# Sliding-window attention: a float32 value product against two passes over split operands, with the output halves added per head

## The reference, cut to what matters

```python
def sliding_window_attention(q, k, v, sinks, slopes):
    ...
    logits = jnp.einsum('bnqkgd,bnskd->bnkgqs', qb, kk).astype(jnp.float32) * scale
    ...
    logits = logits - sl * dist.astype(jnp.float32)
    logits = jnp.where(valid[None, :, None, None], logits, -jnp.inf)
    ...
    p = jax.nn.softmax(jnp.concatenate([logits, sink], axis=-1), axis=-1)[..., :-1]
    out = jnp.einsum('bnkgqs,bnskd->bnqkgd', p.astype(v.dtype), vv)
    return out.reshape(b, s, SW_WIDTH)

def odd_layer(h, w_in, b_in, sinks, w_out):
    ...
    o = sliding_window_attention(q, k, v, sinks, alibi_slopes(SW_HEADS))
    return (o * jax.nn.silu(g)) @ w_out
```

## Time and profile before

| what | value |
|---|---|
| median of 3 runs | 1840.45 us (1839.17 to 1842.74) |
| profiled execution, its time | 1845.26 us |
| its span in the profile | 1843.5 us |
| PE (TensorE matmul) busy over the span | 1673.8 us (91%) |
| DVE (VectorE) busy | 1060.7 us (58%) |
| ACT (ScalarE) busy | 823.3 us (45%) |
| last attention: first score matmul to end of the last value product | 1647.35 to 1767.69 us |

### The profile page before, as it was taken

One profiled execution on the slowest core, in us unless ns is written; L12 is line 12 of the kernel. 1 busy time (PEld: TensorE's weight loads), 2 busy tenths in 40 slices (PEclk: granted clock), 3 DMA queues, 4 the chain that ended last, 5 costly groups with the idle time before them and its releaser, 6 DMA issues.

```text
span 1843.5 us, 24067 instructions
## 1 busy us (share of the span) xinstructions
PE 1673.8 (91%) x8860; PEld 1412.3 (77%) x8860; DVE 1060.7 (58%) x1760; ACT 823.3 (45%) x1544; POOL 93.4 (5%) x112
## 2 busy tenths in 40 slices
PE   7998999998999999989999998889987979979977
PEld 6886787886778888868798896668765758859965
DVE  5557877674545656552254438864465984446654
ACT  5545665663334455541132226652353542235641
POOL 2000400000000000000000001100000100000001
PEclk9998999999999999999999999988997989989988
DMA  6411122113431333322223320111320111320011
GB/s 184 125 50 30 46 63 64 46 52 110 141 120 47 101 104 91 91 92 67 99 74 99 108 81 25 35 46 41 102 84 21 47 46 47 99 69 24 28 42 46
DMA packets 147870, 132.95 MB, mean 72 GB/s; under 512 B 8560, under 2 KB 142448, under 8 KB 147776
## 3 DMA queue, kind: packets, MB, share of 16 engines
q1 hardware_dynamic: 143744, 119.58, 21.3%
q0 software_dynamic: 3136, 10.78, 1.6%
q10 hardware_dynamic: 896, 1.32, 0.3%
HBM read 124.33 MB, written 7.34 MB: 71 GB/s over the span
## 4 chain that ended last, share of the span: by engine, by line
PE 74%; DVE 15%; ACT 5%; issue 5%; DMA 1%; DVEq 0%; ACTq 0%; POOL 0%
PE bank L292 19%; PE bank L293 19%; PE bank L294 19%; DVE wlo L285 2%; PE bank L1206 2%; PE bank L1220 2%; ACT whi L278 1%; PE bank L1189 1%; PE bank L2911 1%; DVE ptl L1374 1%; DVE sz L2700 1%; PE bank L2870 1%; PE bank L1223 1%; PE bank L2278 1%; PE bank L2883 1%
## 5 line engine op out<-in xcount | busy, mean ns | idle before, releaser
L292 PE MATMUL bank<-hh,whi 128*128 128x512 f32 (+3 forms) x1208 | 466.2, 386 | 16.0 <-DVE wlo L285 5.6
L293 PE MATMUL bank<-hl,whi 128*128 128x512 f32 (+3 forms) x1208 | 455.7, 377 | 0.0
L294 PE MATMUL bank<-hh,wlo 128*128 128x512 f32 (+3 forms) x1208 | 455.2, 377 | 0.0
L278 ACT ACTIVATE whi<-wraw 128x2048 fp32r<-128x2048 f32 x111 | 212.1, 1913 | 338.6 <-PE bank L294 338.5
L285 DVE TENSOR_TENSOR wlo<-wraw,whi 128x2048 fp32r<-128x2048 f32 x111 | 254.1, 2289 | 178.7 <-ACT whi L278 177.3
L292 PEld LDWEIGHTS bank<-hh,whi 128*128 128x128 f32 (+2 forms) x1208 | 231.2, 191 | 60.9 <-issue 5.8
L294 PEld LDWEIGHTS bank<-hh,wlo 128*128 128x128 f32 (+2 forms) x1208 | 230.5, 191 | 43.3
L293 PEld LDWEIGHTS bank<-hl,whi 128*128 128x128 f32 (+2 forms) x1208 | 231.2, 191 | 39.1 <-issue 0.7
L1374 DVE TENSOR_TENSOR ptl<-bank,pth 128x128 fp32r<-128x128 f32 (+3 forms) x128 | 56.8, 485 | 64.4 <-ACT pth L1282 63.0
L292 PE MATMUL bank<-ah,whi 128*128 128x512 f32 (+1 forms) x224 | 83.8, 374 | 10.6 <-DVE al L3046 8.3
L292 PE MATMUL bank<-yh,whi 128*128 128x512 f32 (+1 forms) x220 | 79.3, 360 | 6.7 <-DVE yl L1740 6.7
(11 more groups left out here) (393 smaller groups left out, 3212.2 us busy)
## 6 DMA issues: line engine op xcount, KB each, us to landing
wraw<-in_w_in_a_dram SPq DMA_DIRECT2D x52, 512.0 KB, 4.5
wraw<-in_w_up_dram SPq DMA_DIRECT2D x42, 512.0 KB, 4.9
wraw<-in_w_in_dram SPq DMA_DIRECT2D x34, 512.0 KB, 4.8
wraw<-in_w_in_c_dram SPq DMA_DIRECT2D x18, 512.0 KB, 4.7
wraw<-in_w_down_dram SPq DMA_DIRECT2D x16, 512.0 KB, 4.0
wraw<-in_w_out_a_dram SPq DMA_DIRECT2D x16, 512.0 KB, 4.0
aside<-stage POOLq DMA_DIRECT2D x20, 256.0 KB, 2.3
wraw<-in_w_attn_br_dram SPq DMA_DIRECT2D x8, 512.0 KB, 4.0
```

The costliest lines, as they stand in the source:

```text
L278: act.activation(whi[:, p], wraw[:, p], ACT.Copy).then_inc(w_hi_done, 1)
L292: pe.matmul(out, ws[0], hs[0], start=first, stop=False)
L293: pe.matmul(out, ws[0], hs[1], start=False, stop=False)
L294: return pe.matmul(out, ws[1], hs[0], start=False, stop=last)
```

## The change

The value product is made of high and low parts as well. `pth3` and `ptl3` hold the high and low part of the transposed probabilities, `vhl3` holds for each group 64 columns of high values and 64 columns of low values side by side. One pass with `pth3` and one with `ptl3`, both over the same 128 columns, leave in bank 6 the product with the high values in rows 0 to 63 and the product with the low values in rows 64 to 127. ScalarE copies the lower rows to `osum3` (`out_half`), VectorE adds the upper rows to them into `q3` (`out_sum`); this is done for each head, not for each pair. ScalarE now makes all of `pth3` (blocks of 384 and of 512 columns), VectorE all of `ptl3`. `queries_low` and the new `out_sum` stand ahead of the `ptl3` subtractions in VectorE's list, `out_half` stands ahead of the `pth3` copies in ScalarE's. For the odd heads the slope has no low part, and its 4 matmuls and its `dg3` copy are left out. In `window_kv` one VectorE instruction adds the value bias in place of four, the values are split there (two copies, two subtractions), and GpSimd's filling of `vp3` with zeros is gone. In two places a wait of VectorE on its own result and a semaphore raised from there are replaced by a direct wait of the engine that needs the result (`dt_v`, `k3_done`).

```diff
@@ window_kv
+            act.wait_ge(drained, m0 + 2)
+            for g in range(2):
+                act.activation(vhl3[:, :, g, 0:HD], v3[:, :, HD * g:HD * g + HD], ACT.Copy).then_inc(v3_high, 1)
...
-            for tt in range(TT):
-                dst = vp3[:, tt, HD:HD + 256].rearrange("p (g e) -> p g e", g=2)[:, :, 0:HD]
-                ins = dve.tensor_tensor(dst, bank[1][:, P * tt:P * tt + P].rearrange("p (g d) -> p g d", g=2),
-                                        bv3[:, :].rearrange("p (g d) -> p g d", g=2), ALU.add)
-            ins.then_inc(drained, 1)
+            dve.tensor_tensor(v3[:, :, :], bank[1][:, :].rearrange("p (t d) -> p t d", t=TT),
+                              bv3[:, :].unsqueeze(1).to_broadcast([P, TT, P]), ALU.add).then_inc(drained, 1)
+            for g in range(2):
+                dve.wait_ge(v3_high, g + 1)
+                dve.tensor_tensor(vhl3[:, :, g, HD:P], v3[:, :, HD * g:HD * g + HD], vhl3[:, :, g, 0:HD].bitcast(F32),
+                                  ALU.subtract).then_inc(v3_low, 1)
@@ window_attention, TensorE
+        TURNED = ((0, 0, 3 * P), (1, 3 * P, 4 * P))
+        def exact(h):
+            return high_part(sl[h]) == sl[h]
...
-                    pe.matmul(out, dg3[:, h % 2, 0, :], dist3[:, lo:2 * P], start=False, stop=False)
-                    pe.matmul(out, dg3[:, h % 2, 1, :], dist3[:, lo:2 * P], start=False, stop=True).then_inc(s_done, 1)
+                    mm = pe.matmul(out, dg3[:, h % 2, 0, :], dist3[:, lo:2 * P], start=False, stop=exact(h))
+                    if not exact(h):
+                        mm = pe.matmul(out, dg3[:, h % 2, 1, :], dist3[:, lo:2 * P], start=False, stop=True)
+                    mm.then_inc(s_done, 1)
...
-                pe.wait_ge(t3_act, h + 1)
-                pe.wait_ge(t3_dve, h + 1)
-                if e == 0 and hp:
-                    pe.wait_ge(o3_out, hp)
+                pe.wait_ge(t3_dve, 2 * h + 2)
+                if h:
+                    pe.wait_ge(o3_out, h)
...
-                    mm = pe.matmul(bank[6][:, P * j:P * j + n], vp3[:, j, c0:c0 + P],
-                                   pt3[:, h % 2, 2 * P * j:2 * P * j + n], start=(e == 0 and j == 0),
-                                   stop=(e == 1 and j == TT - 1), skip_group_check=True)
+                    for p in (pth3, ptl3):
+                        mm = pe.matmul(bank[6][:, P * j:P * j + n], vhl3[:, j, g, :],
+                                       p[:, h % 2, 2 * P * j:2 * P * j + n], start=(j == 0 and p is pth3),
+                                       stop=(j == TT - 1 and p is ptl3), skip_group_check=True)
@@ window_attention, ScalarE
-            def out_pair(hp):
-                act.wait_ge(pv_done, V3 + 2 * hp + 2)
-                act.activation(q3[:, hp, :], bank[6][:, :], ACT.Copy).then_inc(o3_out, 1)
+            def out_half(h):
+                rows = slice(HD * (h % 2), HD * (h % 2) + HD)
+                act.wait_ge(pv_done, V3 + h + 1)
+                if h >= 2:
+                    act.wait_ge(o3_out, h - 1)
+                act.activation(osum3[rows, :], bank[6][HD:P, :], ACT.Copy).then_inc(o3_half, 1)
...
+                if h >= 2:
+                    out_half(h - 2)
                 if 1 <= h <= NH:
                     v = h - 1
-                    act.wait_ge(t_done, T3 + 2 * v + 1)
                     if v >= 2:
                         act.wait_ge(pv_done, V3 + v - 1)
-                    act.activation(pt3[:, v % 2, 0:3 * P], bank[4][:, 0:3 * P], ACT.Copy).then_inc(t3_act, 1)
-                if h % 2 and h >= 3:
-                    out_pair(h // 2 - 1)
+                    for b, c0, n in TURNED:
+                        act.wait_ge(t_done, T3 + 2 * v + b + 1)
+                        act.activation(pth3[:, v % 2, c0:c0 + n], bank[4 + b][:, 0:n], ACT.Copy).then_inc(t3_act, 1)
                 if h % 2 == 0 and h // 2 + 1 < NH // 2:
                     queries_high(h // 2 + 1)
@@ window_attention, VectorE
+            def out_sum(h):
+                rows = slice(HD * (h % 2), HD * (h % 2) + HD)
+                dve.wait_ge(o3_half, h + 1)
+                dve.tensor_tensor(q3[rows, h // 2, :], bank[6][0:HD, :], osum3[rows, :], ALU.add).then_inc(o3_out, 1)
...
-                    dve.wait_ge(t_done, T3 + 2 * v + 2)
+                if h % 2 == 0 and h // 2 + 1 < NH // 2:
+                    queries_low(h // 2 + 1)
+                if h >= 2:
+                    out_sum(h - 2)
+                if 1 <= h <= NH:
                     if v >= 2:
                         dve.wait_ge(pv_done, V3 + v - 1)
-                    dve.tensor_copy(pt3[:, v % 2, 3 * P:7 * P], bank[5][:, :]).then_inc(t3_dve, 1)
-                if h % 2 == 0 and h // 2 + 1 < NH // 2:
-                    queries_low(h // 2 + 1)
+                    for b, c0, n in TURNED:
+                        dve.wait_ge(t3_act, 2 * v + b + 1)
+                        dve.tensor_tensor(ptl3[:, v % 2, c0:c0 + n], bank[4 + b][:, 0:n],
+                                          pth3[:, v % 2, c0:c0 + n].bitcast(F32), ALU.subtract).then_inc(t3_dve, 1)
```

More of the change, by code:

```diff
@@ L2348, in two_blocks @@
     b_id, b_conv, b_silu = sem("b_id"), sem("b_conv"), sem("b_silu")
-    dt_v, dt_a, cs_done, cs_t, cs_tok, cl_mm, cl_exp = (
-        sem("dt_v"), sem("dt_a"), sem("cs_done"), sem("cs_t"), sem("cs_tok"), sem("cl_mm"),
+    dt_a, cs_done, cs_t, cs_tok, cl_mm, cl_exp = (
+        sem("dt_a"), sem("cs_done"), sem("cs_t"), sem("cs_tok"), sem("cl_mm"),
         sem("cl_exp"))
@@ L2418, in _ @@
             ach(act, act.activation(cshl[:, :], cautf[:, :], ACT.Copy, scale=0.0))
-            act.wait_ge(dt_v, 1)
+            act.wait_ge(drained, m0 + 13)
             ach(act, act.activation(spx[0:SSD_H, :], daf[0:SSD_H, :], ACT.Abs))
@@ L2443, in _ @@
                               ALU.add).then_inc(drained, 1)
-            dve.wait_ge(drained, m0 + 13)
-            dve.sem_inc(dt_v, 1)
             dve.wait_ge(dt_a, 1)
@@ L2760, in two_blocks @@
     sg3 = at("sg3", Y, [KT, S])
-    vp3 = at("vp3", Y + 52 * K, [TT, 320])
-    pt3 = at("pt3", Y + 58 * K, [2, 7 * P])
+    vhl3 = at("vhl3", Y + 52 * K, [TT, 2, P], F32R)
+    osum3 = at("osum3", SC_AT + 12 * K, [S])
+    v3 = at("v3", Y + 28 * K, [TT, P])
+    pth3 = at("pth3", Y + 58 * K, [2, 7 * P], F32R)
+    ptl3 = at("ptl3", SC_AT, [2, 7 * P], F32R)
     bv3 = at("bv3", Y + 66 * K, [P])
@@ L2775, in two_blocks @@
     nsink = at("nsink", S4 + 128, [NH])
-    k3_done, kd3_mm, kd3_done, v3_pad, c4_ready, ns_done = (
-        sem(n_) for n_ in ("k3_done", "kd3_mm", "kd3_done", "v3_pad", "c4_ready", "ns_done"))
+    v3_high, v3_low = sem("v3_high"), sem("v3_low")
+    kd3_mm, kd3_done, o3_half, c4_ready, ns_done = (
+        sem(n_) for n_ in ("kd3_mm", "kd3_done", "o3_half", "c4_ready", "ns_done"))
     dg3_done, t3_act, t3_dve, o3_out = (sem(n_) for n_ in ("dg3_done", "t3_act", "t3_dve", "o3_out"))
@@ L2790, in _ @@
             sp.dma_start(dist3f[:, :], con[:, CCOL["dist2"]:CCOL["dist2"] + 256]).then_inc(got_con, 16)
[L2792 to L2795, removed]
         @block.tensor
@@ L2805, in _ @@
             pe.wait_ge(got_con, CON4)
-            pe.wait_ge(k3_done, 1)
+            pe.wait_ge(drained, m0 + 1)
             for g in range(2):
@@ L2856, in _ @@
             pe.wait_ge(kd_low, 10)
+            pe.wait_ge(v3_low, 2)
             pe.wait_ge(drained, m1)
@@ L2879, in turn @@
                     if i % 2 == 0 and h:
-                        pe.wait_ge(t3_dve if i else t3_act, h)
+                        pe.wait_ge(t3_dve, 2 * h if i else 2 * h - 1)
                     for j in ([0] if i == 0 else [i - 1, i]):
@@ L2901, in values @@
             def values(h):
-                e, hp, g = h % 2, h // 2, h // 8
-                pe.wait_ge(t3_act, h + 1)
-                pe.wait_ge(t3_dve, h + 1)
-                if e == 0 and hp:
-                    pe.wait_ge(o3_out, hp)
-                c0 = HD + P * g if e == 0 else P * g
+                g = h // 8
+                pe.wait_ge(t3_dve, 2 * h + 2)
+                if h:
+                    pe.wait_ge(o3_out, h)
                 for j in range(TT):
                     n = 2 * P if j < TT - 1 else P
-                    mm = pe.matmul(bank[6][:, P * j:P * j + n], vp3[:, j, c0:c0 + P],
-                                   pt3[:, h % 2, 2 * P * j:2 * P * j + n], start=(e == 0 and j == 0),
-                                   stop=(e == 1 and j == TT - 1), skip_group_check=True)
+                    for p in (pth3, ptl3):
+                        mm = pe.matmul(bank[6][:, P * j:P * j + n], vhl3[:, j, g, :],
+                                       p[:, h % 2, 2 * P * j:2 * P * j + n], start=(j == 0 and p is pth3),
+                                       stop=(j == TT - 1 and p is ptl3), skip_group_check=True)
                 mm.then_inc(pv_done, 1)
@@ L2932, in diag @@
                 hi_ = high_part(sl[h])
```

(8 more changed lines are left out.)

3 lines of the change are left out of this document (removed).

## The result

The changed kernel takes 1860.1 us (median of 4, 1857.85 to 1862.32) against 1841.6 us, a ratio of 1.0095 (95% interval 1.0079 to 1.0112): it is 0.8 to 1.1% slower, +18.5 us at the medians. The median of before is 1841.6 with a fourth run, 1.15 above the 1840.45 of the three that the forecast stood on. The last attention grew from 120.3 us (first score matmul to the end of the last value product, 1647.35 to 1767.69) to 137.6 (1641.93 to 1779.52), +17.2. The work behind it takes 76.5 against 75.8.

The account below looks back on a forecast made before the run. The prediction took TensorE as full before and the serial ScalarE and VectorE chain between row maxima as the bound after. +13.4 - 1.3 + 3.6 for half clock - 0.2 gave +15.5 on 1840.45: 1856 us, range 1848 to 1862.

Parts of the forecast that it names:

- The bound: Last attention before the change: TensorE full, 6.90 us a head, with a ScalarE and VectorE chain of little cover.
- 8.10 us: Even step before the change: distance between ends of row maxima, read as the chain of ScalarE and VectorE.
- 9.53: Even step after the change: ScalarE's 5.05 us plus VectorE's 4.48 in series, from row maxima to row maxima.
- 0.5 us of cover: Even step before the change: the scaling of head 4 ends at 1689.51, its transposes start at 1690.02.
- The main term: Row maxima of head 2 to those of head 14: 98.2 us against 84.8 before, +13.4.
- The clock: TensorE falling to half clock after new waits: two of six pairs of heads assumed, +3.6 us; all six +10.8.
- 7.5: Odd step at TensorE's half clock: TensorE's way takes 7.5 us, 1.8 over the chain's 5.74.
- The rest: Outside heads 2 to 14: 0 ahead of head 2, -1.3 us behind head 14, and 0.2 off for small gains.
- 0.96: Value product of one head on TensorE: eight matmuls at 0.12 us take 0.96 in place of 1.51.
- (a): Rival: TensorE stays the bound in the last attention, so the full 12.6 us is gained, 1828 us; chance 0.05.
- (c): Rival: TensorE's clock falls in nearly every pair of heads and stays down, +10.8 us, 1863 us; chance 0.13.

Follow-up runs that it names:

- e4: The kernel before with only the shorter odd heads (low pass of the distance term and its ScalarE copy left out): 1839.7 us, ratio 0.9992.
- e7: The kernel before with the shorter odd heads and the queries' high part made ahead of ScalarE's wait for the row maxima: 1833.8 us, ratio 0.9955.
- e6: The kernel before with only the queries' high part moved ahead of ScalarE's wait for the row maxima: 1838.9 us, ratio 0.9978.
- e10: The changed kernel with spare TensorE matmuls inside both of its waits, ahead of even heads' transposes and odd heads' value product: 1858.6 us, ratio 1.0082.
- e2: The changed kernel without the value product's pass over the low part of the probabilities, 4 of 8 matmuls per head: 1863.4 us, ratio 1.0118.
- e3: The changed kernel with 4 spare TensorE matmuls ahead of the gate part of each even head: 1860.4 us, ratio 1.0097.
- e5: The changed kernel with the queries' high part ahead of ScalarE's row-maxima wait and VectorE's weight item right behind the scaling: 1827.7 us, ratio 0.9932.
- e1: The changed kernel with the queries' high part moved ahead of ScalarE's wait for the row maxima: 1832.8 us, ratio 0.9957.
- e11: The changed kernel once more with nothing edited: 1859.6 us, ratio 1.0089.

## Why the prediction was right

The forecast was 1856 with a range of 1848 to 1862; the median is 1860.1, 18.5 above before where +15.5 was foreseen, and the stage grew by 17.2 where 15.7 was. By its steps:

**The bound.** That TensorE was full was right: in e4 and e7 it stays full, and in e6 the move that gains 27 us in the changed kernel gains 4. The reading of "8.10 us" as the chain of ScalarE and VectorE was not: 1.10 of it is the wait for the transposes in the earlier trace rows, and without it the round takes 6.87. This did no harm to the sum, since 9.53 was added up without that wait and set against the measured 84.8; but "0.5 us of cover" is only the cover of what stands behind the `pt3` copy.

**The main term.** "+13.4" for heads 2 to 14 came out as 102.65 - 84.82 = 17.8, of which about 0.9 is put down to half clock: 10.06 and 10.07 for two even steps in place of 9.90, and 10.48 for step 2, where TensorE comes late out of the half clock at the start (10.49 in e10 too; the kernel before has 8.58 there, 8.09 in e4). At full clock it is 16.9. The mechanism was right, its terms were too small: the even step is 9.90 and not 9.53, the odd ones 5.96 and 8.16 and not 5.74 and 7.94, 6 x 0.37 + 6 x 0.22 = 3.5. The forecast let each instruction overlap the next by 0.1. The rows of after show no overlap on either side of `out_half` and ahead of `out_sum`: the gate copy starts at 1712.75 and the next at 1713.38, `out_half` at 1713.38 and the next at 1713.99, 0.63 and 0.61 for the assumed 0.48 each; `queries_low` to `out_sum` takes 1.42 for 1.31. These three make 0.39 us, which is the 0.37 that the even step was short of. Why they do not overlap is open. A wait in front is not enough for it: before, `out_pair` and the `pt3` copy have one too and start 0.39 and 0.47 behind instructions of 0.49 and 0.61 (1690.94 and 1697.68).

**The clock.** "+3.6", two of six pairs at 1.8, was oversized. The waits are followed by half clock three times from head 3 on in the profiled execution, but in steps 5, 9 and 13, where VectorE's weight item sets the pace (8.16 stays 8.16), and the next even step then costs 0.16. The forecast did not ask on which step the half clock falls. e10 takes nearly all of it away and gains 0.3 in the stretch. Where the half clock meets an odd step without an item it mostly costs 0.9 (e2, e3), half of the 1.8 (6.85 for "7.5"). The two errors, 3.5 too little and about 2.7 too much, nearly cancelled, and that was luck.

**The rest.** The end of the stage was -0.6 where -1.3 stood, the start 0 as forecast. TensorE's waits are 1.08 to 1.65 and 1.64 where "some 1 us" and 1.8 stood; VectorE's wait for the queries is 3.95 (some 3). The value product came out at 0.87, not 0.96: the last two matmuls, of 128 columns, start 0.06 apart. The rule of the Trainium skill that the forecast weighed (TensorE: Matmul & The Clock Gate, Back-to-back issue gap), which that section gives for the isolated gap of a single matmul and not for a stream with weight loads, gave 0.77; the run lies between the two. How much TensorE saves plays no part in the result (e2). What was put at nothing or at 0.2 ahead of the stage can't be told from the varying start of the stage (see the end).

**The rivals.** (a), TensorE stays the bound, did not come for this order of the lists. It was right about something else: with two moves the same instructions run in 105.4 us of stage (e5). Its full 12.6 us on a stage of 120.3 would be 107.7; e5 goes below that because the early queries also save 3.2 us in the first step and 2.3 in the second (e6), though TensorE still idles for 3.7 us of the stage. (c), half clock in nearly every pair for 10.8 us, did not come: behind the start it followed in three of six pairs and cost 0.3, which is what e10 gains without it.

## What to carry to other kernels

- When work is taken off a full engine, write down the loop of waits between the others from one end of a product to the next, in the order of their lists, before counting the gain. Take the waits for the full engine out of that loop: here a step of 8.10 us was a loop of 6.87 and a wait, and 3.0 us was put into it.
- An instruction that depends on nothing new belongs ahead of the engine's longest wait, not behind the copies of the step. The move of two ScalarE copies is worth 27 us in one kernel and 4 us in the other, and in an even step it takes off more than twice what the copies last, 3.6 us: the price of a place in the list is set by what stands in series behind it.
- e5, the change with two moves, is 0.5 to 0.9% faster than the kernel before, and the split value product's own share in e1 against e7 is 1.9 us of stage.

## What was not expected

- The last two matmuls of the value product, both of 128 columns, start 0.06 us apart, while float32r matmuls of 128 columns took 0.10 to 0.14 in the scores of both kernels. That the two share their weights is not the reason: the high and low key pass of the scores share theirs (`qs3`) as well and start 0.14 apart (1713.33 and 1713.47). The cause is open.
- Taking TensorE work away (e2) made the profiled stage 1.1 us longer, with half clock in steps where it lies on the path. Whether a wait of 1.6 to 2.1 us is followed by half clock differs from step to step in one execution, and it falls on other steps in e2 and e3 than in the changed kernel and e11. What decides it was not tried.
- The code ahead of the stage is the same in all these kernels but for a few instructions, and the first score matmul started at 1640.8 to 1648.1 us in 13 profiled executions. The changed kernel's profile began it 5.4 us earlier than that of before, so that the spans differ by 12.5 us only, and the stage by 17.2. Why the start varies is open; parts of a trace are better compared by stage than by span.
